# Two hybrid layers of a fused network: convolution inputs projected first, and VectorE's work in the projection stage dealt out unit by unit

## The reference, cut to what matters

```python
z = rmsnorm(x, mix_norm) @ w_in
(aq, ak, av, iq, ik, iw, bq, bk, bv, bg, br, cu, dcq, dckv, dkpe) = split(z)

# a: attention over the keys that an indexer picks
s = relu(einsum('bthd,bsd->bths', iqb, ik) * idx_scale)      # 8 index heads of 32
score = einsum('bths,bth->bts', s, wb)                       # weighted sum over the heads
score = where(causal, score, -inf)
_, sel = top_k(score, 128)                                   # of up to 512 keys, for each query
y_a = attention of aq over the selected keys, with a bias by distance

# b: gated linear attention from bq, bk, bv, bg, br
# c: convolution
a, gate = split(cu, 2)                                       # 256 channels each
h = a * sigmoid(gate)
h = depthwise_conv(h, w_dw, 31 taps, causal) + b_dw
y_c = silu(rmsnorm(h, c_norm))
# d: latent attention from dcq, dckv, dkpe, 4 heads, with rmsnorm and rope for each head's q and k

x = x + concatenate([y_a, y_b, y_c, y_d]) @ w_out
```

## Time and profile before

| | |
|---|---|
| median of 3 runs | 3637.14 us (3636.79 to 3638.01) |
| the profiled execution | 3634.32 us, its span 3632.3 us |
| granted TensorE clock, mean over the span | 0.965 of full speed |
| TensorE busy | 3447.4 us, 95% |
| VectorE busy | 1590.7 us, 44% |
| ScalarE busy | 1168.1 us, 32% |
| GpSimd busy | 567.8 us, 16% |

### The profile page before, as it was taken

The page is one execution under the profiler, slowest core; times in us unless marked ns, Lnnn a source line. Parts: engine busy times, 40 slices in busy tenths (PEclk is TensorE's granted clock), DMA queues, the critical chain, the costliest instruction groups (busy, mean ns, idle before and its releaser), DMA issues.

```text
span 3632.3 us, 39887 instructions
## 1 busy us (share of the span) xinstructions
PE 3447.4 (95%) x14476; PEld 2614.1 (72%) x14476; DVE 1590.7 (44%) x2227; ACT 1168.1 (32%) x1720; POOL 567.8 (16%) x361
## 2 busy tenths in 40 slices
PE   7999998899999999999799999899899998889998
PEld 5888763677888788766477888566678886568886
DVE  3332388534333333258644332744343326464322
ACT  4332334433322332244334321213333213543322
POOL 1110233111100110033311110401011003321100
PEclk9999998899999999999699999899999999899999
DMA  4332321023333333322003333331123332223332
GB/s 132 97 93 93 81 76 36 1 64 93 92 95 93 90 94 97 91 72 71 1 24 92 92 93 96 95 74 47 47 81 92 95 96 64 70 70 92 93 97 76
DMA packets 420124, 286.04 MB, mean 79 GB/s; under 512 B 57416, under 2 KB 395180, under 8 KB 419884
## 3 DMA queue, kind: packets, MB, share of 16 engines
q1 hardware_dynamic: 419200, 283.62, 26.9%
q10 hardware_dynamic: 828, 1.13, 0.1%
HBM read 280.24 MB, written 4.47 MB: 78 GB/s over the span
## 4 chain that ended last, share of the span: by engine, by line
PE 87%; DVE 8%; ACT 2%; issue 2%; POOL 0%; DMA 0%; DVEq 0%; ACTq 0%; SPq 0%; POOLq 0%
PE bank L842 24%; PE bank L843 24%; PE bank L844 24%; PE bank L1226 1%; PE bank L1109 1%; PE bank L1110 1%; PE bank L1128 1%; PE bank L837 1%; DVE arena L2024 1%; PE bank L1220 1%; DVE arena L2003 1%; DVE small L2000 1%; DVE w_lo L1908 0%; PE bank L979 0%; PE bank L978 0%
## 5 line engine op out<-in xcount | busy, mean ns | idle before, releaser
L844 PE MATMUL bank<-xn_lo,w_hi 128*128 128x512 f32 x2800 | 1100.9, 393 | 0.0
L842 PE MATMUL bank<-xn_hi,w_hi 128*128 128x512 f32 x2496 | 1000.4, 401 | 58.9 <-DVE xn_lo L1897 20.1
L843 PE MATMUL bank<-xn_hi,w_lo 128*128 128x512 f32 x2496 | 991.0, 397 | 0.0
L1908 DVE TENSOR_TENSOR w_lo<-wring,w_hi 128x1024 fp32r<-128x1024 f32 x434 | 542.1, 1251 | 898.7 <-ACT w_hi L1474 897.6
L1474 ACT ACTIVATE w_hi<-wring 128x1024 fp32r<-128x1024 f32 x490 | 518.0, 1060 | 1187.2 <-DMA wring<-in_ffn_down 357.7
L844 PEld LDWEIGHTS bank<-xn_lo,w_hi 128*128 128x128 f32 x2800 | 530.9, 190 | 133.1
L842 PEld LDWEIGHTS bank<-xn_hi,w_hi 128*128 128x128 f32 x2496 | 470.8, 189 | 181.6 <-issue 63.9
L843 PEld LDWEIGHTS bank<-xn_hi,w_lo 128*128 128x128 f32 x2496 | 471.8, 189 | 104.2 <-issue 1.7
L843 PE MATMUL bank<-h_hi,w_lo 128*128 (+1 forms) x1056 | 420.4, 398 | 0.0
L842 PE MATMUL bank<-h_hi,w_hi 128*128 (+1 forms) x1056 | 415.8, 394 | 0.0
L844 PE MATMUL bank<-h_lo,w_hi 128*128 (+1 forms) x1056 | 415.2, 393 | 0.0
(11 more groups left out here) (372 smaller groups left out, 3173.1 us busy)
## 6 DMA issues: line engine op xcount, KB each, us to landing
wring<-in_ffn_gate SPq DMA_DIRECT2D x88, 512.0 KB, 3.8
wring<-in_ffn_up SPq DMA_DIRECT2D x88, 512.0 KB, 3.8
wring<-in_ffn_down SPq DMA_DIRECT2D x88, 512.0 KB, 3.5
wring<-in_ffn_w_gate SPq DMA_DIRECT2D x44, 512.0 KB, 3.8
wring<-in_ffn_w_up SPq DMA_DIRECT2D x44, 512.0 KB, 3.8
wring<-in_ffn_w_down SPq DMA_DIRECT2D x44, 512.0 KB, 3.6
wring<-in_w_in SPq DMA_DIRECT2D x34, 512.0 KB, 3.7
wring<-in_w_out SPq DMA_DIRECT2D x16, 512.0 KB, 4.4
```

The costliest lines, as they stand in the source:

```text
L842: nc.tensor.matmul(ps, w_hi[:, slot, t, 0:M], hi, start=start, stop=False)
L843: nc.tensor.matmul(ps, w_lo[:, slot, t, 0:M], hi, start=False, stop=False)
L844: return nc.tensor.matmul(ps, w_hi[:, slot, t, 0:M], lo, start=False, stop=stop)
L1908: nc.vector.tensor_tensor(w_lo[:, slot, :, :].rearrange("p k c -> p (k c)"), wunit[:, slot, :], w_hi[:, slot, :, :].rearrange("p k c -> p ...
```

## The change

The labels are put in another order: `cg0`, `ca0`, `cg1`, `ca1` first, then the index and the other projections. Three lists say what stands at which unit: how many index matmuls behind a label (`Z_IDX`), how many convolution steps VectorE runs (`Z_TAPS`, all 62 in this stage), and how many top-k rounds (`Z_ROUNDS`, 20 of 48 in this stage). `w_lo` is made by VectorE (`dve_units`, L1908), no longer by GpSimd. For unit n VectorE makes `w_lo`, runs the unit's convolution steps, then the scores of the index matmuls behind label n - 2, then the unit's rounds (`dve_z`). The steps go through the first channel tile and then through the second, each waiting for the step before it; the first step of a tile waits for that tile's product alone. The 28 other rounds stand in the head loop, four to a head, where the convolution steps stood.

```diff
-Z_LABELS = ["iq0", "iq1", "ik", "misc", "aq0", "aq1", "ak0", "ak1", "br0", "br1", "cg0", "cg1", "ca0", "ca1", "dcq0", "dcq1",
-            "dckv", "bq", "bk"]
+Z_LABELS = ["cg0", "ca0", "cg1", "ca1", "iq0", "iq1", "ik", "misc", "aq0", "aq1", "ak0", "ak1", "dcq0", "dcq1", "dckv",
+            "br0", "br1", "bq", "bk"]
...
+Z_IDX = [0] * 8 + [3, 3] + [2] * 9
+Z_TAPS = [0] * 4 + [6] * 6 + [4] * 5 + [3] * 2 + [0] * 6
+Z_ROUNDS = [0] * 17 + [3] * 4 + [4] * 2
...
-    if _u >= 4:
-        for _ in range(2):
-            if _left:
-                Z_SEQ.append(("idx",) + _left.pop(0))
+    for _ in range(Z_IDX[_u]):
+        Z_SEQ.append(("idx",) + _left.pop(0))
...
-                act.e.wait_ge(conv.h, conv.by(act.l, 2 * TAPS - 1 + ct))
+                act.e.wait_ge(conv.h, conv.by(act.l, TAPS * (ct + 1)))
...
-        def dve_index(dve):
...
+        def dve_scores(dve, first, end):
+
+            for ni in range(first, end):
+                tb, h = IDX_UNITS[ni]
+                dve.e.wait_ge(z_sb.h, z_sb.by(dve.l, IDX_POS[ni] + 1))
...
+        def dve_top(dve, first, end):
+
+            for nt in range(first, min(end, 3 * TOP_N)):
+                tb, r = 3 - nt // TOP_N, nt % TOP_N
+                if r:
+                    dve.e.wait_ge(top_rep.h, top_rep.by(dve.l, nt))
+                else:
+                    dve.e.wait_ge(idx_mask.h, idx_mask.by(dve.l, 4 - tb))
+                nc.vector.max(m8, score(tb)).then_inc(top_max.h, 1)
+                dve.e.wait_ge(top_max.h, top_max.by(dve.l, nt + 1))
+                nc.vector.match_replace(score(tb), m8, score(tb), SENTINEL).then_inc(top_rep.h, 1)
...
         def dve_conv(dve, first, end):
 
-            if first == 0:
-                dve.e.wait_ge(hp_ready.h, hp_ready.by(dve.l, 2))
-            for n in range(first, min(end, 2 * TAPS)):
-                j, ct = n // 2, n % 2
-                w = cur_dw[:, n:n + 1]
+            for n in range(first, end):
+                ct, j = n // TAPS, n % TAPS
+                if j == 0:
+                    dve.e.wait_ge(hp_ready.h, hp_ready.by(dve.l, ct + 1))
+                w = cur_dw[:, 2 * j + ct:2 * j + ct + 1]
...
-                    dve.e.wait_ge(conv.h, conv.by(dve.l, n - 1))
+                    dve.e.wait_ge(conv.h, conv.by(dve.l, n))
...
+        def dve_z(dve, st):
+
+            ni = nc_ = nt = 0
+            for n in range(2, NZU):
+                dve_units(dve, st, n, n + 1)
+                dve_conv(dve, nc_, nc_ + Z_TAPS[n])
+                nc_ += Z_TAPS[n]
+                if 0 <= n - 2 < len(Z_LABELS):
+                    dve_scores(dve, ni, ni + Z_IDX[n - 2])
+                    ni += Z_IDX[n - 2]
+                dve_top(dve, nt, nt + Z_ROUNDS[n])
+                nt += Z_ROUNDS[n]
+
+        HEAD_TOP = sum(Z_ROUNDS)
+        HEAD_PART = -(-(3 * TOP_N - HEAD_TOP) // 9)
...
-                dve_conv(dve, CONV_EARLY + i * CONV_PART, CONV_EARLY + (i + 1) * CONV_PART)
+                dve_top(dve, HEAD_TOP + i * HEAD_PART, HEAD_TOP + (i + 1) * HEAD_PART)
...
-                dve_index(dve)
-                dve_conv(dve, 0, CONV_EARLY)
+                dve_z(dve, z)
...
-        def pool_z(pool, st):
-            for n in range(2, NZU):
-                pool_units(pool, st, n, n + 1)
-                for ct in range(2):
-                    if n == Z_LABELS.index(f"ca{ct}") + 3:
-                        pool.e.wait_ge(z_sb.h, z_sb.by(pool.l, max(Z_POS[f"ca{ct}"], Z_POS[f"cg{ct}"]) + 1))
-                        nc.gpsimd.tensor_tensor(hpad[:, ct, TAPS - 1:], T(t_ca[ct]), T(t_cg[ct]),
-                                                ALU.mult).then_inc(hp_ready.h, 1)
+        def pool_z(pool):
+            for ct in range(2):
+                pool.e.wait_ge(z_sb.h, z_sb.by(pool.l, max(Z_POS[f"ca{ct}"], Z_POS[f"cg{ct}"]) + 1))
+                nc.gpsimd.tensor_tensor(hpad[:, ct, TAPS - 1:], T(t_ca[ct]), T(t_cg[ct]), ALU.mult).then_inc(hp_ready.h, 1)
```

More of the change, by code:

```diff
@@ L172 @@
 IDX_UNITS = [(tb, h) for tb in (3, 2, 1) for h in range(IDX_HEADS)]
+Z_IDX = [0] * 8 + [3, 3] + [2] * 9
+Z_TAPS = [0] * 4 + [6] * 6 + [4] * 5 + [3] * 2 + [0] * 6
+Z_ROUNDS = [0] * 17 + [3] * 4 + [4] * 2
+assert len(Z_IDX) == len(Z_LABELS) and sum(Z_IDX) == len(IDX_UNITS)
+assert len(Z_TAPS) == len(Z_ROUNDS) == NZU and sum(Z_TAPS) == 2 * TAPS
 Z_SEQ = []
@@ L2008, in program @@
-        CONV_EARLY = 31
-        CONV_PART = -(-(2 * TAPS - CONV_EARLY) // 9)
-        def dve_conv(dve, first, end):
-            if first == 0:
-                dve.e.wait_ge(hp_ready.h, hp_ready.by(dve.l, 2))
-            for n in range(first, min(end, 2 * TAPS)):
-                j, ct = n // 2, n % 2
-                w = cur_dw[:, n:n + 1]
+        def dve_scores(dve, first, end):
+            for ni in range(first, end):
+                tb, h = IDX_UNITS[ni]
+                dve.e.wait_ge(z_sb.h, z_sb.by(dve.l, IDX_POS[ni] + 1))
+                w = wA[:, tb * 8 + h:tb * 8 + h + 1]
+                r = idx_r[ni % 4][:, 0:(tb + 1) * P]
+                if h == 0:
+                    ins = nc.vector.tensor_scalar(score(tb), r, w, None, ALU.mult)
+                else:
+                    dve.e.wait_ge(idx_acc.h, idx_acc.by(dve.l, ni))
+                    ins = nc.vector.scalar_tensor_tensor(out=score(tb), in0=r, scalar=w, in1=score(tb),
+                                                         op0=ALU.mult, op1=ALU.add)
+                ins.then_inc(idx_acc.h, 1)
+                if h == IDX_HEADS - 1:
+                    dve.e.wait_ge(idx_acc.h, idx_acc.by(dve.l, ni + 1))
+                    dg = score(tb)[:, tb * P:]
+                    nc.vector.tensor_tensor(dg, dg, C("causal"), ALU.add).then_inc(idx_mask.h, 1)
@@ new lines, in program @@
+        TOP_N = TOPK // 8
+        def dve_top(dve, first, end):
[3 more added lines that the diff above has]
+                    dve.e.wait_ge(top_rep.h, top_rep.by(dve.l, nt))
+                else:
+                    dve.e.wait_ge(idx_mask.h, idx_mask.by(dve.l, 4 - tb))
+                nc.vector.max(m8, score(tb)).then_inc(top_max.h, 1)
+                dve.e.wait_ge(top_max.h, top_max.by(dve.l, nt + 1))
+                nc.vector.match_replace(score(tb), m8, score(tb), SENTINEL).then_inc(top_rep.h, 1)
+                if r == TOP_N - 1:
+                    dve.e.wait_ge(top_rep.h, top_rep.by(dve.l, nt + 1))
+                    nc.vector.tensor_scalar(score(tb), score(tb), 0.9 * SENTINEL, NEG, ALU.is_gt, ALU.mult).then_inc(top_done.h, 1)
@@ L2646, in _ @@
                 pool_pairs(pool, turn(3 * l + 1))
-                pool_z(pool, STAGES["in", l])
+                pool_z(pool)
                 pool_mixers(pool)
```

## The result

The changed kernel takes 3614.45 us (median of four executions, 3610.73 to 3621.25) against 3637.12 us of the kernel before (3636.79 to 3638.01): a ratio of 0.9939, 95% interval 0.9926 to 0.9952. The forecast was 3617.3 us with a range of 3609 to 3629. The time is right; the experiments show that one of its reasons is not.

What follows compares the result with a forecast made beforehand. The prediction took TensorE as the bound (87% of the chain, VectorE 8%). Terms of -16.5 (stage) and -3.3 (head loop) gave -19.8 us: 3634.3 - 19.8 + 2.8 = 3617.3 us, range 3609 to 3629.

Steps and rivals of the forecast that it cites:

- (1): Projection stage, both layers: top-k rounds leave the middle of the scores, TensorE's stall goes, -17.3 us; -16.5 after a charge.
- (2): Projection stage: new order of projections costs TensorE 0 and ScalarE 0 to 0.5 us, including later loads of "misc".
- (3): Projection stage: weight parts go from GpSimd to VectorE, 26.3 us of VectorE's time per layer; cost to the total 0.
- 98% full: Projection stage: VectorE's work sums to 123.6 us, which just fits the time TensorE gives it.
- The limit of 8 us: Projection stage: a weight part from VectorE may be about 8 us late before TensorE waits.
- (4): Head loop of the mixers: top-k rounds replace convolution steps, 1.6 us gained per layer, -3.3 us in all.
- the walk: Head-loop estimate with half-clock stretches placed as in the trace: 46.0 and 43.7 us, against 47.7 and 45.8.
- A: Rival, projection stage: VectorE becomes the bound, 5.5 us more per layer at 1.0 us a step, 3628 us; chance 0.15.
- B: Rival, projection stage: VectorE misses so far that TensorE waits and its clock falls, 3663 us; chance 0.05.
- D: Rival, projection stage: rounds at units 17 to 20 close the relu buffers again, half the stall returns, 3626 us; chance 0.04.
- C: Rival, head loop: the stage gains but the loop doesn't, half clock covers the short heads, about 3624 us; chance 0.13.

Runs made afterwards that it cites:

- experiment 1: The kernel before with nine relu buffers instead of four for the index scores: 3639.77 us, ratio 1.0006.
- experiment 2: The kernel before with nine relu buffers and without the 31 convolution steps between VectorE's last top-k round and the mixers: 3619.87 us, ratio 0.9955.
- experiment 5: The changed kernel with one, then three, tiny VectorE copies ahead of each chained convolution step: 3617.89 us and 3616.07 us.
- experiment 3: The changed kernel with the 21 weight parts of each hybrid layer back on GpSimd: 3627.77 us, ratio 0.9973.
- the other trace: Profile of the changed kernel run once more, unchanged, a long execution (span 3619.6 against 3609.0 us); median of that run 3615.56 us, ratio 0.9941.

## Why the prediction was right, and where it was not

- *The term of TensorE's stall* (-17.3 in (1)): the stage became 9.9 and 8.8 us shorter, and experiments 1 and 2 give 16 us when VectorE is free. Right in size, wrong as stated: "The stall has then no cause: -17.3 us" took the stage's end for TensorE's alone. The row was there: 29 of the 31 steps in 19.29 us, and the first step of the mixers starts right behind them (the rows in experiment 1). I used that row for a price only. What makes the term real is the rest of the change, which I had costed at 0: VectorE ends its stage work at 555 us instead of 572. I said of the changed kernel that nothing waits there, and that is right (5.75 us idle), but I never asked it of the kernel before. So the price of the stall came out right by luck: both conditions lay in the same change.
- *(2) Order of projections*: no wait for the weights of "misc" nor for its banks shows in the stage; right.
- *(3) Weight parts on VectorE*: prices right (1.22 for 1.25 us, steps 0.785 for 0.79, rounds as priced). "98% full" was too much: VectorE is busy 108.9 of the 129 us from 422 to 551 us, the scores of 256 and 384 keys cost 0.48 and 0.62 us, not 0.79, and experiment 5 put 10.8 us more on VectorE for nothing. The limit of 8 us for a late part was too low as well: the last part of the changed kernel is taken up 10.8 us after ScalarE's half, and no matmul waits. What I missed is the other side: I took the relief from GpSimd into the price of a step, but set only the 26.3 us against TensorE's time and 0 as the move's worth. Beside GpSimd the same work costs VectorE 34 us more; experiment 3 has the move at 13 us of the total.
- *(4) Head loop*: -3.3 forecast, -5.9 in the profiled execution (-4.7 and +0.8 in the two layers of the other trace). VectorE sets the loop, as the walk had it; between the two executions, with different granted clocks, a layer's loop differs by 1.5 and 3.4 us.
- *Given back*: 2.7 us between the head loop and the next norm, not in the sum, and 1.3 us gained ahead of layer 0; the cause of neither was looked for. In the profiled execution: 18.7 + 5.9 + 1.3 - 2.7 = 23.2 us against a forecast of 19.8.
- *The rivals*: A and B did not come (no wait for a weight part in the stage), D neither. C did not come in the profiled execution; in the long one the loop of layer 1 gains nothing. The missing rival was the one that experiment 1 shows: the stall is removed and VectorE's end takes its place, 3637 us. It would have come, by the rows of experiment 1, if the convolution steps had stayed behind the last round; that was not run.

## What to carry to other kernels

Before a stall is priced as its length, look at what the next stage waits for: if another engine works there without a gap up to the next stage's first step, the stall hides that engine's lateness, and removing it alone brings nothing (experiment 1). A two-input elementwise operation given to GpSimd is not off VectorE's account when VectorE's own queue is full of such operations: here each took 1.6 us of it on average, against 1.22 us for doing it on VectorE. Work that nobody waits for goes where the timeline shows an engine idle, not into a loop in which it is the slowest; that alone gave another 18 us.

## What the runs showed of the hardware that I had not expected

- A one-input TENSOR_SCALAR of 128x256 took 2330 ns beside a weight part of 2.4 us on GpSimd (350 ns alone); MAX8 took 692 ns in both.
- A chained step cost 0.785 us and an alternating one 0.665; a tiny copy (147 to 152 ns busy) put between them added only 0.06 us, and three of them 0.18, so each adds less than half of its own busy time.
- The same program, in two executions, had granted clocks of 0.67 and 0.72 in the head loop of layer 1, and 0.95 and 1.00 in the last 67 to 70 us ahead of the next norm, 3 us each time.
